# A two-block transformer kernel: rotary turn by small transfers, merged score tails, full bias rows, and a final projection in products of 512 columns

## The reference, cut to what matters

```python
q = apply_partial_rope(q.reshape(B, T, 8, 64), cos, sin)   # k likewise
# of each 64 channels the first 16 turn: x1 = xr[:8], x2 = xr[8:16]
# rot = [x1 * c - x2 * s, x2 * c + x1 * s]; the other 48 stay
scores = einsum('bqhmd,bkhmd->bhmqk', q, k) * 64 ** -0.5   # 4 heads, m = 2 maps
p = softmax(where(cid[q] >= cid[k], scores, -inf))         # chunks of 64 tokens
w = p[:, :, 0] - lam * p[:, :, 1]
o = rms_norm(w @ v, subln_w) * (1 - lam_init)
mixed = concat([o * silu(g_att), lru_out])                 # 512 + 512 channels
out = rms_norm(h + mixed @ w_out, final_norm_w)[:, 16:]
```

## Time and profile before

| what | value |
| --- | --- |
| median of three timed runs | 3039.01 us (3038.16 to 3039.3) |
| the profiled execution, its own time | 3038.45 us |
| its span, first to last instruction | 3036.6 us |
| mean granted TensorE clock | 0.995 of full speed |

### The profile page before, as it was taken

How to read it: one execution, slowest core, us unless ns; L and a number is a source line. 1 busy time by engine, 2 the same in 40 slices (tenths; PEclk the granted TensorE clock), 3 DMA queues, 4 the chain that set the end, 5 groups by cost and what they waited for, 6 DMA issues and landing times.

```text
span 3036.6 us, 39147 instructions
## 1 busy us (share of the span) xinstructions
PE 2963.1 (98%) x16315; PEld 2508.6 (83%) x16315; DVE 1558.2 (51%) x2184; ACT 1072.9 (35%) x2306; POOL 371.4 (12%) x437
## 2 busy tenths in 40 slices
PE   7999999999999999999999999999999999999998
PEld 5788888888888888888878888888888888888887
DVE  5466566667664224131257454544454488633553
ACT  4443444454443213233432341112112244313553
POOL 0122231332231000000000000000000022001111
PEclk9999999999999999999999999999999999999999
DMA  3211111111012111111353321111111141101101
GB/s 120 73 53 46 46 49 49 46 42 36 26 41 70 46 62 45 58 42 56 122 223 128 112 88 63 44 54 42 56 42 56 45 147 56 56 28 67 39 29 43
DMA packets 59649, 193.37 MB, mean 64 GB/s; under 512 B 7728, under 2 KB 15536, under 8 KB 50256
## 3 DMA queue, kind: packets, MB, share of 16 engines
q1 hardware_dynamic: 58464, 189.26, 18.1%
q10 hardware_dynamic: 1008, 1.61, 0.2%
HBM read 156.86 MB, written 33.98 MB: 63 GB/s over the span
## 4 chain that ended last, share of the span: by engine, by line
PE 86%; DVE 7%; ACT 3%; issue 1%; DMA 1%; SPq 1%; POOL 0%; ACTq 0%; POOLq 0%; DVEq 0%
PE ps L2532 22%; PE ps L2534 22%; PE ps L2533 22%; PE ps L745 3%; PE ps L751 3%; PE ps L1759 1%; PE ps L3422 1%; PE ps L1722 1%; PE ps L757 1%; PE ps L782 1%; PE ps L776 1%; PE ps L788 1%; PE ps L728 1%; PE ps L797 1%; PE ps L796 1%
## 5 line engine op out<-in xcount | busy, mean ns | idle before, releaser
L2532 PE MATMUL ps<-r,r 128*128 128x512 f32 (+4 forms) x2992 | 1170.8, 391 | 20.7 <-DVE ar L3673 5.1
L2534 PE MATMUL ps<-r,r 128*128 128x512 f32 (+4 forms) x2992 | 1112.2, 372 | 0.0
L2533 PE MATMUL ps<-r,r 128*128 128x512 f32 (+4 forms) x2992 | 1109.8, 371 | 0.0
L2532 PEld LDWEIGHTS ps<-r,r 128*128 128x128 f32 (+1 forms) x2992 | 563.3, 188 | 113.1 <-issue 16.7
L2534 PEld LDWEIGHTS ps<-r,r 128*128 128x128 f32 (+1 forms) x2992 | 561.1, 188 | 99.8
L2533 PEld LDWEIGHTS ps<-r,r 128*128 128x128 f32 (+1 forms) x2992 | 563.6, 188 | 81.0 <-issue 2.5
L2532 PE MATMUL ps<-r 128*128 128x512 f32 x512 | 199.7, 390 | 0.8 <-DVE r L2521 0.8
L2534 PE MATMUL ps<-r 128*128 128x512 f32 x512 | 199.2, 389 | 0.0
L2533 PE MATMUL ps<-r 128*128 128x512 f32 x512 | 199.2, 389 | 0.0
L2793 DVE TENSOR_TENSOR ar<-ar,ps 128x512 f32<-128x512 f32 x224 | 150.8, 686 | 89.7 <-PE ps L2534 89.6
L2516 ACT ACTIVATE r<-ar 128x2048 fp32r<-128x2048 f32 x48 | 91.7, 1910 | 268.1 <-PE ps L2534 252.3
(11 more groups left out here) (331 smaller groups left out, 3927.0 us busy)
## 6 DMA issues: line engine op xcount, KB each, us to landing
ar<-wst SPq DMA_DIRECT2D x72, 1024.0 KB, 4.8
ar<-wst SPq DMA_DIRECT2D x56, 512.0 KB, 4.1
ar<-x SPq DMA_DIRECT2D x16, 512.0 KB, 5.7
ar<-sc_g SPq DMA_DIRECT2D x32, 256.0 KB, 4.6
sc_h<-ar SPq DMA_DIRECT2D x32, 256.0 KB, 2.0
sc_x<-ar SPq DMA_DIRECT2D x16, 512.0 KB, 2.8
ar<-sc_x SPq DMA_DIRECT2D x16, 512.0 KB, 3.9
sc_b<-ar SPq DMA_DIRECT2D x24, 260.0 KB, 2.0
```

The source lines that it names most:

```text
L2532: t.do.matmul(o, l[0], r[0], start=first, stop=False)
L2533: t.do.matmul(o, l[0], r[1], start=False, stop=False)
L2534: return t.do.matmul(o, l[1], r[0], start=False, stop=last)
```

## The change

Five edits, and the names that go with them:

1. **Rotary turn.** The permutation products leave PE, with `permT`, its table and its load. ACT, behind each copy, waits for its own copy and issues four transfers SBUF to SBUF of 8 partitions each (rows 0 to 7 and 8 to 15 of either 64 change places) from `rp` to `rturn`; DVE multiplies `rturn` with a sine table that now holds the signs. POOL fills `rturn` with zeros before.
2. **Score tails.** `scores` cuts at every 512 only, and the mask product adds to the last 64 columns of the longer product.
3. **Bias rows.** The bias products are 128 partitions deep instead of 33 (the rows behind are zero).
4. **Final projection.** A product takes 512 columns, 256 out of each of two weight places, by a hand-built access pattern (`fin_weights`); the places stay where they were. A step does one half of the 8 contractions of one column half (`late_half`), so `rows_add` comes every second step with 512 columns; the pieces between the transposes of the late steps become 2, 1 and 1 of 4 contractions (were 3, 3 and 2 of 8).
5. **Names.** The last weight loads write a tensor of their own name at the same place, and `rope_in` is folded into `lru_in`.

```diff
-                t.do.matmul(bank(6 + n % 2)[:, 0:384], bc(rb[0:33, n:n + 1], 33, 128), oh[0:33, n // 4, :], start=True, stop=True).then_inc(*bias_mm.tick(n))
+                t.do.matmul(bank(6 + n % 2)[:, 0:384], bc(rb[:, n:n + 1], 128, 128), oh[:, n // 4, :], start=True, stop=True).then_inc(*bias_mm.tick(n))
...
+        rturn = [A(vO + 3104 + 512 * i, 512) for i in range(2)]
...
-            t.do.matmul(rope_bank(k)[:, 0:w], permT, rp[i % 2][:, 0:w], start=True, stop=True).then_inc(*rope_mm.tick(k))
...
         def pe_rope(t):
-            for k in rope_keys[:2]:
-                rotated(t, k)
-            for i, _ in enumerate(begun["k"]):
-                rotated(t, rope_keys[2 + i])
-            for i, _ in enumerate(pe_cols3(t, "q", 0, (1, 2))):
-                rotated(t, rope_keys[10 + i])
+            for _ in begun["k"]:
+                pass
+            for _ in pe_cols3(t, "q", 0, (1, 2)):
+                pass
...
                 a.do.activation(rp[i % 2][:, 0:w], of_bank(k)[:, 0:w], ACT.Copy, scale=0.125 if k[0] == "q" else 1.0).then_inc(*pj_act.tick(k))
+                if i < 2:
+                    a.wait_ge(filled, "mask")
+                a.wait_ge(pj_act, k)
+                for s_, (to, of) in enumerate(((0, 8), (8, 0), (64, 72), (72, 64))):
+                    a.do.dma_start(rturn[i % 2][to:to + 8, 0:w], rp[i % 2][of:of + 8, 0:w]).then_inc(*rope_turned[i % 2].tick((*k, s_)))
...
-                v.wait_ge(rope_in, "sin")
-                v.wait_ge(rope_mm, k)
-                v.do.tensor_tensor(d, rope_bank(k)[:, 0:w], sinT[:, pos:pos + w], ALU.mult).then_inc(*rope_dve.tick(("sin", *k)))
+                v.wait_ge(lru_in, "sin")
+                v.wait_ge(filled, "mask")
+                v.wait_ge(rope_turned[i % 2], (*k, 3))
+                v.do.tensor_tensor(d, rturn[i % 2][:, 0:w], sinT[:, pos:pos + w], ALU.mult).then_inc(*rope_dve.tick(("sin", *k)))
...
-                    if (sl, i) == (0, 0):
-                        rotated(t, rope_keys[-2])
                     if (sl, i) == (0, 1):
-                        rotated(t, rope_keys[-1])
                         stage_left(t, "pe", 7)
...
+        def fin_weights(cp, kt):
+            near = [fin_pairs[cp][:, SLOT * part + 256 * kt:SLOT * part + 256 * kt + 256] for part in range(2)]
+            return [bass.AP(x_.tensor, x_.offset, [x_.ap[0], [FIN_STEP[cp], 2], [1, 256]]) for x_ in near]
...
-                    cuts += [(k0, k1)] if k1 <= lo or k0 >= lo else [(k0, lo), (lo, k1)]
+                    cuts.append((k0, k1))
...
-                            o = t.do.matmul(dst[m], negr[rows_, :], oner[rows_, 0:k1 - k0], start=False, stop=True)
+                            o = t.do.matmul(dst[m][:, max(lo - k0, 0):], negr[rows_, :], oner[rows_, 0:k1 - max(lo, k0)], start=False, stop=True)
...
-                i, cb = fin_of(n)
-                wv = w_parts(JF0 + cb, 8)
-                t.wait_ge(w_lo, JF0 + cb)
+                i, cp, late_half = fin_of(n)
+                t.wait_ge(w_lo, JF0 + 1 + 2 * cp)
                 t.wait_ge(mix_lo, i if i < 6 else (i, "lru"))
-                if n - 6 and not k0:
-                    t.wait_ge(y_sum, fin_of(n - 1))
-                for k in range(k0, k1):
+                if n - 6 and not late_half and not k0:
+                    t.wait_ge(y_sum, fin_of(n - 1)[0:2])
+                for k in range(4 * late_half + k0, 4 * late_half + k1):
...
-            def rows_add(i, cb):
-                y = YF[i % 2][:, 256 * cb:256 * cb + 256]
+            def rows_add(i, cp, late_half):
+                if not late_half:
+                    return
+                y = YF[i % 2][:, 512 * cp:512 * cp + 512]
...
         def pool_mask(p):
+            p.do.memset(rturn[0], 0.0)
+            p.do.memset(rturn[1], 0.0).then_inc(*pool_step.tick())
```

More of the change, by code:

```diff
@@ L124, in program @@
         wins = {}
[L125 removed]
+        for off, n in ([(0, 8192), (39488, 8192), (0, 8320), (39488, 8320), (12416, SLOT), (14464, SLOT), (47808, SLOT), (49856, SLOT), (17920, 128), (12416, 31168), (43584, 8320), (8320, SLOT), (10368, SLOT)] + [(1024 * i, 1024) for i in range(8)]
                        + [(39488 + 1024 * i, 1024) for i in range(8)] + [(SLOT * i, SLOT) for i in (4, 5, 6, 7, 13, 14, 15, 16, 17, 18)]
@@ L133, in program @@
                     wins[off, n] = c2.enter_context(nc.sbuf_tensor(f"r{off}_{n}", [P, n], F32R))
+        last_stage = []
+        for i in range(2):
+            with ExitStack() as c2:
+                c2.enter_context(nc.sbuf_tensor(f"before_last{i}", [P, 8320 + SLOT * i], F32))
+                last_stage.append(c2.enter_context(nc.sbuf_tensor(f"last_stage{i}", [P, SLOT], F32)))
         ar = ctx.enter_context(nc.sbuf_tensor("ar", [P, NAR], F32))
@@ L2490, in program @@
         Q0 = 26624
-        SETF = [SETS[0]] + [(R_(39488 + 4096 * i, SLOT), R_(41536 + 4096 * i, SLOT)) for i in range(2)] + [SETS[1]]
+        fin_pairs, FIN_STEP = (R_(12416, 31168), R_(43584, 8320)), (39488 - 12416, 47808 - 43584)
+        SETF = [tuple(fin_pairs[c // 2][:, FIN_STEP[c // 2] * (c % 2) + SLOT * part:][:, 0:SLOT] for part in range(2)) for c in range(4)]
         NJ, JF0 = NW - W2, 44
@@ L2882, in program @@
         GT = [A(Q0 + 10456 + 532 * i, 512) for i in range(2)]
-        lru_in = flow("lru_in", ["conv"] + [(g, n) for g in range(2) for n in range(8)], 16)
+        lru_in = flow("lru_in", ["conv", "lqk"] + [(g, n) for g in range(2) for n in range(8)] + ["cos", "sin"], 16)
         coef_a, coef_v = flow("coef_a", ["abs", "exp", "ln", "lam"]), flow("coef_v", ["rate", "sum", "lam"])
@@ L2936, in program @@
         lru_a = [flow(f"lru_a{q}", [(ct, n) for ct in (q, q + 2) for n in ("a", "th", "sqrt")]) for q in range(2)]
-        rope_mm = flow("rope_mm", rope_keys)
+        rope_turned = [flow(f"rope_turned{q}", [(*k, s_) for k in rope_keys[q::2] for s_ in range(4)], 16) for q in range(2)]
         rope_dve = flow("rope_dve", [(n, *k) for k in rope_keys for n in ("sin", "out")])
@@ L3256, in sp_rope @@
             for n, key, dst in ((0, "cos", cosT), (1, "sin", sinT)):
-                sp.do.dma_start(dst, rope[n]).then_inc(*rope_in.tick(key))
+                sp.do.dma_start(dst, rope[n]).then_inc(*lru_in.tick(key))
             for j in range(38, 42):
@@ L3334, in program @@
         ysum = [st4[:, 64 + 2 * i:66 + 2 * i] for i in range(8)]
-        fin_keys = [(i, cb) for i in i8 for cb in range(4)]
+        fin_keys = [(i, cp) for i in i8 for cp in range(2)]
         mix_hi, mix_lo = [flow(n, [*range(6), *PIECES_LATE]) for n in ("mix_hi", "mix_lo")]
@@ L3459, in final @@
                         t.wait_ge(mix_lo, (i, "heads"))
-                    o = mm3(t, fin_bank(i, cb), [m_[:, kt, :] for m_ in late.get(i, m2)], [w_[:, kt, :] for w_ in wv], k == 0, k == 7)
-                if k1 == 8:
-                    o.then_inc(*y_mm.tick((i, cb)))
+                    o = mm3(t, fin_bank(i, cp), [m_[:, kt, :] for m_ in late.get(i, m2)], fin_weights(cp, kt), k == 0, k == 7)
+                if late_half and k1 == 4:
+                    o.then_inc(*y_mm.tick((i, cp)))
             def last_rows(piece):
@@ L3467, in last_rows @@
                 t.wait_ge(mix_lo, (7, piece))
-                for cb in range(4):
-                    t.wait_ge(w_lo, JF0 + cb)
-                    wv = w_parts(JF0 + cb, 8)
+                for cp in range(2):
                     for kt in range(k0, k1):
-                        o = mm3(t, fin_bank(7, cb), [m_[:, kt, :] for m_ in late[7]], [w_[:, kt, :] for w_ in wv], kt == 4, kt == 3)
+                        o = mm3(t, fin_bank(7, cp), [m_[:, kt, :] for m_ in late[7]], fin_weights(cp, kt), kt == 4, kt == 3)
                     if piece == "end":
-                        o.then_inc(*y_mm.tick((7, cb)))
+                        o.then_inc(*y_mm.tick((7, cp)))
             def values(n):
@@ L3509, in pe_diff @@
                 turn(n - 2)
-                final(n, 0, 3)
+                final(n, 0, 2)
                 next(groups)
-                final(n, 3, 6)
+                final(n, 2, 3)
                 next(groups)
                 values(n - 1)
-                final(n, 6, 8)
+                final(n, 3, 4)
             for n in range(N - 2, N):
@@ L3519, in pe_diff @@
                 next(groups)
-                final(n, 0, 3)
+                final(n, 0, 2)
                 turn(n - 2)
                 next(groups)
-                final(n, 3, 6)
+                final(n, 2, 3)
                 next(groups)
                 values(n - 1)
-                final(n, 6, 8)
-            final(N, 0, 4)
+                final(n, 3, 4)
+            final(N, 0, 2)
             turn(N - 2)
-            final(N, 4, 8)
+            final(N, 2, 4)
             values(N - 1)
```

42 lines of the change are left out of this document (16 added, 26 removed).

## The result

| | before | changed |
| --- | --- | --- |
| median, us | 3039.16 (3038.16 to 3039.99, 4 runs) | 3015.89 (3014.65 to 3018.21, 4 runs) |
| ratio, 95% interval | | 0.9927 [0.9914, 0.9939] |
| the profiled execution, its own time, us | 3038.45 | 3018.21 |

What follows compares the result with a forecast made beforehand. PE, busy 98% of the span, was taken to bound the kernel, with gaps set by DVE and ACT in the last stage. Turn -13.8, bias -2.2 and walk -5.3 gave -21.3 us from 3039.0: 3017.7 us, range 3010 to 3026.

Steps and rivals of the forecast that it cites:

- The turn: Rotary stage, second block: twenty permutation products leave a PE that is never idle there, -13.8 us.
- the loop: Rotary stage: a buffer is free again after copy, four issues, landing and three DVE passes, 6.0 us (6.4 for a query).
- the limit is about 10 us. The margin over 6.4 us is 3.6 us: Rotary stage: longest buffer loop that PE's pace and four-bank lead hide, about 10 us, against 6.4 us for a query.
- The rival on the other side: Rotary stage: late transfer landings make the loop set the pace; kernel slower than before, .05 (the loop has .04 of it).
- The bias rows: First stage: 128-deep products gain .40 us each; five on the chain and half of another count, -2.2 us (0 to -4.8).
- The others lie behind such a wait and I count none: First stage: the remaining bias products stand behind a wait like the chain's DMA transfer of 4.99 us and gain nothing.
- The tails: Score products: one cut less per item saves .144 us on the mean, 4.6 us over 32 items.
- the walk: Scores and final projection, 2786 us to the end, step by step: -5.3 us of the 9.7 us freed on PE.
- the groups of four: Steps 10 to 25: four groups of four steps, each gaining .47 us, -1.9 us in all.
- one step where ACT ends last gives only its .14: Steps 10 to 25: in each group, the step where ACT ends last gains only the shorter score tail, .14 us.
- From step 26 on: Last steps: smaller pieces and longer add +.5, add wait before step 31 -.6, merged matmuls -.96, shorter tails; about -1.8 us.
- the .27: Scores and final projection: steps with DVE's 512-column add have .27 us more; a group's step where DVE ends last loses it.

Runs made afterwards that it cites:

- turn6: Changed kernel with two of the four turn transfers of each piece cut in two, so six issues a piece; 3027.45 us, ratio 0.9965.
- bias64: Kernel before with bias products 64 partitions deep (33 before, 128 in the changed kernel); 3038.33 us, ratio 0.9997.
- bias_only: Kernel before with the bias rows 128 partitions deep alone; 3033.24 us, ratio 0.9984.
- final_only: Kernel before with the final projection in products of 512 columns alone; 3038.29 us, ratio 1.0003.
- tails_only: Kernel before with the merged score tails alone; 3036.06 us, ratio 0.9992.
- turn8: Changed kernel with all four turn transfers of each piece cut in two, so eight issues a piece; 3046.03 us, ratio 1.0026.

## Why the prediction was right, and where it was not

**The turn: right, -13.85 for -13.8**, and the loop of 5.9 us for 6.0, the latter by luck. Its cover was wrong. I put the limit of the loop at 10 us, by the four banks that PE may be ahead. With six issues the loop is some 7.1 us (.46, 3.8, 1.3, 1.5) and 10.6 us are lost. The step that failed is "the limit is about 10 us. The margin over 6.4 us is 3.6 us": I took the cover of the stage's middle for that of its end, where ACT's copies of the values stand behind the barrier. There the changed kernel has an estimated 2.5 us left: in turn6 ACT passes the barrier 10.1 us later against PE's work (2729.8 for 2722.9, and PE 3.25 us earlier), and PE's gaps are 7.6 us. The rival on the other side, slower than before, was thus nearer than forecast: eight issues a piece are enough, though their data land 1.2 us later and not 7.8.

**The bias rows: the mechanism right, the size not, -2.2 forecast.** Over all traces here, the first product of the inverses starts at 119.5 to 121.2 us in the five without the edit and at 112.7 to 116.4 in the nine with it, on the mean 120.0 and 114.4: -5.6 us. Five products give .36 each for .40 forecast (1.8 us between 63 and 82 us). Three between 91 and 99 us give nothing, since the transfer of the gate rows is the path there, as I had argued. The step that failed is "The others lie behind such a wait and I count none": two products lie behind the transfer, at 104 to 107 us, where they gain about .5 us (from the first of them to the third matmul behind it takes 3.88 us in bias64 and 3.42 in bias_only, both at the lower clock), and the clock is higher there, which I had not in the sum at all. From the first of the two to the inverses it takes 14.7 us before, 13.4 in the changed kernel and 11.5 in turn6, where the granted clock from 104 to 112 us is .57, .78 and 1.00; so about .9 and 2.8 us of that go with the clock. It has a second share ahead of the transfer: from the sixth bias product to the seventh, between 82 and 89 us, it takes 5.7 to 5.9 us in four of the five traces without the edit, and 4.3 in bias64 and in the nine with it, where the granted clock is 1.00 there.

Why the clock is higher stays open. It isn't that PE waits less ahead of the two products. That wait, before, in the changed kernel and in turn6:

```profile
104.31 0.66 PE L688 MATMUL ps<-ar 128*128 128x128 f32 x4 [2.16 <-ACT ar L1004]
```
```profile
102.10 1.12 PE L695 MATMUL ps<-ar 128*128 128x128 f32 x4 [3.38 <-ACT ar L1011]
```
```profile
101.03 0.66 PE L695 MATMUL ps<-ar 128*128 128x128 f32 x4 [3.00 <-ACT ar L1011]
```

It is 1.9 to 2.7 us in the five without the edit and 2.9 to 3.5 in the nine with it. The profiled execution of the changed kernel is at the poor end, A 116.36, which goes with its being the longest of the four.

**The tails: right in kind**, -2.5 up to item 24, at most -3.8 in all, for -4.6 if all passed.

**The final projection and the walk: the sum on PE right (.226 us for two places), its worth wrong, -3.5 for -5.3.** At the transposes of the values of items 4, 8 and 24, which PE makes in steps 6, 10 and 26, the changed kernel is ahead by .62, 1.59 and 2.87 us, and at the end by 3.51. The four parts of the walk are thus -.6, -1.0, -1.3 and -.6, for -.55, -1.0, -1.9 and -1.8. Two steps of it failed. In the groups of four, "one step where ACT ends last gives only its .14" gave 0, and the steps with PE last gave .2 to .3 for .30. "From step 26 on", the 72 products behind the last wait did give what was forecast, .96 (26.9 us to the end for 27.9). But the "+.5" up to the end of the first long wait for the add is .85 in final_only (39.2 us from the transpose of item 24, 38.4 before), and the shorter tails, the .7 that is left of the 1.8, give .25 there in tails_only (38.1 us). The -.6 lies between the two long waits: 16.0 us before and 15.9 in the changed kernel, with the lower clock in both, 15.0 in tails_only and 14.5 in final_only without it, so -.1 or -.5. Alone, the final projection gives -.3: in each block the .27 takes back what the two steps with PE last keep, .12 each.

The sum therefore: -13.85, -5.6 and about -3.5 make -23.0, against -23.3 by the medians. That the forecast of -21.3 came so near is partly luck: the bias term was 3.4 us too small and the last one 1.8 too large.

## What to carry to other kernels

Price what hides a new wait at the end of a stage, not in its middle: where an engine's next job stands behind a barrier, a lead of several buffers counts for only what is left there. Before an engine that is 98% busy is given less to do, follow one period of the steps and ask which engine ends last in each; what is saved in front of a wait comes back as a longer wait, and a pass made wider on the engine that ends last is paid in full. Moving work that nobody waits for (the scaling of finished rows) out of the way of the maximum gave 4.3 us up to item 24, more than the 384 merged products; 3.0 of them were lost again where, at the end, a product did wait behind it.

## What was not expected of the hardware

- PE's long waits can be followed by a stretch at the 1.2 GHz level, so they cost more than their length: behind 6.4 us in turn6 the granted clock was .50 for 5 us, 2.8 us more. Behind the same work it differs between executions (.66 and 1.00 in the last part of two kernels that are alike there), and the longer wait does not decide it: behind 2.16 us in the kernel before the granted clock was .57, behind 3.00 in turn6 it was 1.00.
- A float32 product of 384 columns among products 128 deep takes .84 us with 64 partitions as with 33, and holds up the matmul behind it (.43 us); with 128 it takes .65, and the next .23.
- A transfer SBUF to SBUF of 8 partitions took ACT's queue .65 us to issue, one of 4 partitions .61 (4.88 us for eight in turn8), and the data were there 1.2 to 1.3 us after the last issue had ended.
